# Gate logits and output projection with tokens as rows: 512 columns a product, bias folded in by split products

## The reference, cut to what matters

```
proj = rmsnorm(x, ln_mix_g) @ w_in            # q, k, v of two attentions, then ga, gb (1024 each)
o_a, o_b = attention a (512 wide), attention b (256 wide)
mix = sigmoid(ga + b_gate_a) * (o_a @ w_o_a) + sigmoid(gb + b_gate_b) * (o_b @ w_o_b)
x   = x + mix @ w_out
x   = x + moe_ffn(rmsnorm(x, ln_ffn_g))       # router, top 4 of 32 experts, gate/up/down products
return rmsnorm(x, ln_final_g)
```

## Time and profile before

| what | value |
| --- | --- |
| median of 3 executions | 1134.42 us (1134.16 to 1135.12) |
| the profiled execution | 1132.39 us, span of its instructions 1130.4 us |
| mean granted PE clock | 0.998 |
| busy | PE 97%, PE weight load 44%, DVE 28%, ACT 18%, POOL 2% |
| HBM read | 437.69 MB, 388 GB/s over the span |

### The profile page before, as it was taken

How to read it: one execution, slowest core, us unless ns; L and a number is a source line. 1 busy time by engine, 2 the same in 40 slices (tenths; PEclk the granted TensorE clock), 3 DMA queues, 4 the chain that set the end, 5 groups by cost and what they waited for, 6 DMA issues and landing times.

```text
span 1130.4 us, 12440 instructions
## 1 busy us (share of the span) xinstructions
PE 1094.6 (97%) x5385; PEld 496.0 (44%) x5385; DVE 315.7 (28%) x684; ACT 205.4 (18%) x367; POOL 19.6 (2%) x27
## 2 busy tenths in 40 slices
PE   8999999999999999999999999999999999999997
PEld 6888888733333333333333333333333333333332
DVE  7566778421111111111121111111111111111121
ACT  6445547210000000000110000000000000000011
POOL 1000110000000000000000000000000000000000
PEclk9999999999999999999999999999999999999999
DMA  9854229999999999999999999999999999999997
GB/s 360 264 181 156 110 78 407 408 403 429 427 435 419 430 428 427 432 428 431 430 429 431 429 432 427 431 431 430 432 430 433 428 432 430 434 431 430 426 427 286
DMA packets 38727, 439.23 MB, mean 389 GB/s; under 512 B 3050, under 2 KB 4482, under 8 KB 19748
## 3 DMA queue, kind: packets, MB, share of 16 engines
q1 hardware_dynamic: 38388, 438.41, 92.4%
q10 hardware_dynamic: 304, 0.33, 0.1%
HBM read 437.69 MB, written 1.05 MB: 388 GB/s over the span
## 4 chain that ended last, share of the span: by engine, by line
PE 72%; DMA 25%; DVE 1%; issue 1%; ACT 0%; SPq 0%; DVEq 0%; POOLq 0%; POOL 0%; ACTq 0%
PE ps L1150 42%; DMA pair<-in_w_up_dram 21%; PE ps L776 5%; PE ps L1174 5%; DMA pair<-in_w_down_dram 4%; PE ps L1080 3%; PE ps L878 2%; PE ps L806 2%; PE ps L814 2%; PE ps L931 1%; PE ps L1127 1%; PE ps L933 1%; PE ps L932 1%; PE ps L1019 1%; PE ps L1021 1%; PE ps L1020 1%
## 5 line engine op out<-in xcount | busy, mean ns | idle before, releaser
L1150 PE MATMUL ps<-pair,o_t 128*64 128x512 f32 x3072 | 681.0, 595 | 20.6 <-DMA pair<-in_w_gate_dram 16.8
L1150 PEld LDWEIGHTS ps<-pair,o_t 128*64 128x64 f32 x3072 | 215.9, 137 | 441.2 <-issue 408.0
L1624 DVE TENSOR_SCALAR work<-ps 128x512 f32<-128x512 f32 x32 | 22.1, 691 | 492.2 <-PE ps L1150 492.2
L710 ACT ACTIVATE o_t<-ps 128x512 f32<-128x512 f32 x32 | 19.1, 597 | 297.9 <-PE ps L776 297.9
L1174 PE MATMUL ps<-attn,o_t 64*128 64x512 f32 x256 | 71.5, 639 | 0.0
L697 ACT ACTIVATE attn<-work 128x512 f32<-128x512 f32 x32 | 20.1, 629 | 258.4 <-DVE work L1624 258.4
L1080 PE MATMUL ps<-xs,work 128*64 128x512 f32 x256 | 60.9, 593 | 0.0
L716 ACT ACTIVATE attn<-ps 128x512 f32<-128x512 f32 x31 | 18.5, 597 | 228.0 <-PE ps L1150 228.0
L776 PEld LDWEIGHTS ps<-cst,work 128*128 128x128 f32 (+1 forms) x294 | 35.8, 170 | 54.8 <-issue 52.1
L776 PE MATMUL ps<-cst,work 128*128 128x128 f32 (+1 forms) x294 | 53.0, 296 | 1.0 <-DVE work L1441 0.6
L1630 DVE TENSOR_SCALAR a_rows<-ps 128x512 f32<-128x512 f32 x32 | 22.1, 691 | 103.1 <-PE ps L1150 103.1
(11 more groups left out here) (184 smaller groups left out, 841.7 us busy)
## 6 DMA issues: line engine op xcount, KB each, us to landing
pair<-in_w_gate_dram SPq DMA_DIRECT2D x25, 4096.0 KB, 35.3
pair<-in_w_up_dram SPq DMA_DIRECT2D x25, 4096.0 KB, 34.5
pair<-in_w_down_dram SPq DMA_DIRECT2D x25, 4096.0 KB, 36.9
pair<-in_w_gate_dram SPq DMA_DIRECT2D x12, 2048.0 KB, 13.5
pair<-in_w_up_dram SPq DMA_DIRECT2D x12, 2048.0 KB, 15.3
pair<-in_w_down_dram SPq DMA_DIRECT2D x9, 2048.0 KB, 13.3
wd<-in_w_in_dram SPq DMA_DIRECT2D x5, 2048.0 KB, 9.1
wu<-in_w_in_dram SPq DMA_DIRECT2D x4, 2048.0 KB, 11.1
```

Of the source, the lines that this page charges most:

```text
L1150: mm = pe.matmul(ps[SLOTS * h:SLOTS * h + SLOTS, bank, :], lhs[:, k, :], ring[(at + j) % RING][:, r, 512 * h:512 * h + 512], start=(k == 0 ...
```

## The change

Gates: 8 outputs of 128 tokens by 512 gate columns in place of 16 of 128 columns by 256 tokens. Each is filled in two parts (`gate_part(u)`, 4 k steps each), so the place in the weave stays. ACT's emptying of PSUM applies 1/std of the token as its scale, in 8 instructions of 512 columns, after odd u only, and POOL's 16 multiplications go. Since the bias now varies along the columns, it goes in as a first product over 3 rows: std of the token (split hi, hi, lo) by bias (hi, lo, hi), which the later 1/std cancels. For that there are four new DMAs (broadcast to 32 rows each), one ACT copy after chunk 5, four DVE instructions ahead of the first gate, and the first gate waits for them.

Mixer: 4 outputs n of 128 tokens by 512 columns, in an order written out by hand; sigmoids are 4 instructions of 1024 elements. The mix must then be transposed, 4 PE transposes for each n (`turn_mixed`); ACT and DVE split it out of PSUM. Splits of the rows of `w_out` stand at other places of ACT's and DVE's order. The experts' biases are split at u = 2, not 8.

```diff
-            def evac_gate(t):
-                act.wait_ge(gate_done, t + 1)
-                act.activation(gates[:, t // KT, t % KT, :], ps[:, t % 2, 0:SEQ], ACT.Copy).then_inc(gate_read, 1)
+            def evac_gate(i):
+                c, b = i // NB, i % NB
+                act.wait_ge(gate_done, i + 1)
+                if i == 3:
+                    act.wait_ge(bias_lo_ready, 1)
+                act.activation(gates[:, 2 * (c % 2) + b, c // 2, :], ps[:, i % 2, :], ACT.Copy, scale=stat[:, 12 + b:13 + b])\
+                   .then_inc(gate_read, 1)
...
-                evac_gate(u)
+                if u % 2:
+                    evac_gate(u // 2)
...
-                if u == 8:
+                if u == 2:
                     split_biases()
...
-            act.wait_ge(gates_scaled, 16)
...
+            act.wait_ge(gate_read, 8)
             sigmoids(0)
             sigmoids(1)
             act.wait_ge(p_turned, N_UNITS)
             act.wait_ge(ld_wout[0], 16)
             split_row(0)
+            split_row(1)
             sigmoids(2)
...
+            mixed_hi(0)
+            mixed_hi(1)
+            sigmoids(3)
             act.wait_ge(ld_wout[1], 16)
+            act.wait_ge(mix_ready, 2)
             split_row(4)
...
+            def gate_part(u, ks):
+                i, c = u // 2, GATE_CHUNK0 + u // 4
+                b, bank = i % NB, i % 2
+                if ks[0] == 0:
+                    if i >= 2:
+                        pe.wait_ge(gate_read, i - 1)
+                    elif i == 0:
                         pe.wait_ge(proj_read, NB * 7)
+                        pe.wait_ge(gbias_ready, 4)
+                    at = 32 * (c - GATE_CHUNK0)
+                    pe.matmul(ps[:, bank, :], std_tab[at:at + 3, P * b:P * b + P], gbias_tab[at:at + 3, :], start=True, stop=False)
                 for k in ks:
+                    if k % 2 == 0 and b == 0:
+                        pe.wait_ge(hi_ready, PARTS * c + k // 2 + 1)
+                        pe.wait_ge(lo_ready, PARTS * c + k // 2 + 1)
+                    pe.matmul(ps[:, bank, :], h_hi[:, b, k, :], w_hi[:, c % 2, k, :], start=False, stop=False)
+                    pe.matmul(ps[:, bank, :], h_lo[:, b, k, :], w_hi[:, c % 2, k, :], start=False, stop=False)
+                    mm = pe.matmul(ps[:, bank, :], h_hi[:, b, k, :], w_lo[:, c % 4, k, :], start=False, stop=(k == KT - 1))
...
+                gate_part(2 * q, range(0, 4))
...
                 if q + 1 in LATE:
-                    gate_tile(2 * q + 1, range(0, 3))
+                    gate_part(2 * q + 1, range(4, 6))
                     scores(q + 1)
-                    gate_tile(2 * q + 1, range(3, KT))
+                    gate_part(2 * q + 1, range(6, KT))
...
+            def turn_mixed(n):
+                pe.wait_ge(mix_ready, n + 1)
+                for j in range(4):
+                    mm = turn(ps[:, TURNED[n], P * j:P * j + P], mix_rows[n][:, P * j:P * j + P])
+                mm.then_inc(mix_turned, 1)
...
             mixer_a(0)
+            mixer_a(1)
+            mixer_b(0)
+            mixer_b(1)
+            mixer_a(2)
+            turn_mixed(0)
+            turn_mixed(1)
+            mixer_b(2)
+            mixer_a(3)
+            turn_mixed(2)
+            mixer_b(3)
...
+                if k == 0:
+                    turn_mixed(3)
...
+                    dve.wait_ge(spread_ready, 1)
+                    dve.tensor_scalar(std_all, std_hi[:], cst[:, C_SGN + 2:C_SGN + 3], None, ALU.mult).then_inc(gbias_ready, 1)
+                    dve.wait_ge(spread_ready, 2)
+                    dve.tensor_scalar(gbias_s, gbias_hi[:], cst[:, C_SGN + 3:C_SGN + 4], None, ALU.mult).then_inc(gbias_ready, 1)
+                    dve.wait_ge(gbias_ready, 2)
+                    dve.scalar_tensor_tensor(std_tab[:], ps[:, 6, 0:SEQ], cst[:, C_SGN:C_SGN + 1], std_all, ALU.mult, ALU.add)\
+                       .then_inc(gbias_ready, 1)
+                    dve.scalar_tensor_tensor(gbias_tab[:], gbias_raw, cst[:, C_SGN + 1:C_SGN + 2], gbias_s, ALU.mult, ALU.add)\
+                       .then_inc(gbias_ready, 1)
...
-                if u == 8:
+                if u == 2:
                     dve.wait_ge(bias_hi_ready, 1)
...
+            mixed_a(0)
+            split_row(0)
+            mixed_a(1)
+            mixed(0)
+            mixed(1)
+            split_row(1)
+            mixed_a(2)
+            mixed_lo(0)
+            mixed_lo(1)
+            mixed(2)
+            split_row(4)
+            mixed_a(3)
+            mixed(3)
+            mixed_lo(2)
+            split_row(5)
+            split_row(2)
+            mixed_lo(3)
```

More of the change, by code:

```diff
@@ L408, in _ @@
             sp.dma_start(msk, masks).then_inc(ld_msk, 16)
+            for c in range(4):
+                of = (b_gate_a, b_gate_b)[c // 2][0:1, CHUNK * (c % 2):CHUNK * (c % 2) + CHUNK]
+                sp.dma_start(gbias_raw[32 * c:32 * c + 32, :], of.broadcast_to([32, CHUNK])).then_inc(ld_rows, 16)
             for part in range(2):
@@ L633, in _, with sigmoids, mixed_hi @@
             split_hi(N_CHUNKS + 1, 1)
-            act.wait_ge(gates_scaled, 16)
             evac_o(5)
             split_o(5, 6)
[L638 to L641, removed]
+            def sigmoids(n):
+                act.activation(gates[:, n, :, :], gates[:, n, :, :], ACT.Sigmoid).then_inc(gates_ready, 1)
             def split_row(k):
                 act.activation(wx_hi[k], wx_raw[:, k, :], ACT.Copy).then_inc(wx_hi_ready, 1)
+            def mixed_hi(n):
+                act.wait_ge(mix_turned, n + 1)
+                for to, at in turned_parts(n, mix_ha, mix_hb):
+                    act.activation(to, at, ACT.Copy).then_inc(mix_hi_ready, 1)
+            act.wait_ge(gate_read, 8)
             sigmoids(0)
@@ L982, in mixer_product @@
                 for k in tiles:
-                    pe.matmul(ps[:, MIX[m % 4], columns], wo_hi[:, k, P * m:P * m + P], o_hi[:, k, :],
-                              start=(k == tiles[0]), stop=False)
-                    pe.matmul(ps[:, MIX[m % 4], columns], wo_hi[:, k, P * m:P * m + P], o_lo[:, k, :], start=False, stop=False)
-                    mm = pe.matmul(ps[:, MIX[m % 4], columns], wo_lo[:, k, P * m:P * m + P], o_hi[:, k, :],
-                                   start=False, stop=(k == tiles[-1]))
@@ L988, in mixer_product @@
-                return mm
-            def mixer_a(m):
-                if m < 2:
-                    pe.wait_ge(gate_read, 15 + m)
-                elif m >= 4:
-                    pe.wait_ge(mix_ready, m - 3)
-                mm = mixer_product(m, range(0, 4), slice(0, SEQ))
-                if m == KT - 1:
-                    mm.then_inc(oproj_a_done, 1)
+                    pe.matmul(ps[:, bank, :], o_hi[:, k, cut], wo_hi[:, k, half], start=(k == tiles[0]), stop=False)
+                    pe.matmul(ps[:, bank, :], o_lo[:, k, cut], wo_hi[:, k, half], start=False, stop=False)
@@ new lines, in mixer_product, with mixer_a, mixer_b @@
+                    mm = pe.matmul(ps[:, bank, :], o_hi[:, k, cut], wo_lo[:, k, half], start=False, stop=(k == tiles[-1]))
+                return mm
+            def mixer_a(n):
+                if n == 0:
+                    pe.wait_ge(gate_read, 7)
+                elif n >= 2:
+                    pe.wait_ge(mix_a_used, n - 1)
+                mixer_product(n, range(0, 4), MIX[n % 2][0]).then_inc(oproj_a_done, 1)
+            def mixer_b(n):
+                if n == 0:
+                    pe.wait_ge(gate_read, 8)
+                    pe.wait_ge(lo_ready, PARTS * (N_CHUNKS + 1) + 2)
+                    pe.wait_ge(o_lo_ready, 2)
+                elif n == 1:
+                    pe.wait_ge(o_ready, 6)
+                else:
+                    pe.wait_ge(mix_ready, n - 1)
+                mixer_product(n, range(4, 6), MIX[n % 2][1]).then_inc(oproj_done, 1)
```

166 lines of the change are left out of this document (76 added, 90 removed).

## The result

The changed kernel takes 1141.16 us (median of 4, 1140.21 to 1141.90) where the kernel before takes 1134.29 in the same comparison: a ratio of 1.0062 (95% interval 1.0049 to 1.0074), 6.9 us slower. I had forecast 1135.8 and a range up to 1138.8. The profiled execution took 1140.99 us.

A forecast was written before the change was run, and what follows sets the result against it. The DMA weight stream sets the end, which follows the first expert product. Terms 0.3 (last gate) + 0.2 + 0.4 (mixer) + 0.5 (output product) = +1.4 us on 1134.42 gave 1135.8, range 1132.8 to 1138.8.

The forecast's parts named there:

- the DMA hides it: Rival: DMA backlog carries the PE's delay and only the last gate's +0.3 us counts, 1134.7; chance 0.1.
- the price of the bias product's neighbourhood: Gate tiles: weight change between the 3-row bias product and its neighbours, bounds 0 and 0.10 us, taken as 0.05.
- The wide product saves the cover of one load a tile: Gate tiles: a wide first product may cover the weight load, saving 0 to 0.1 us a tile, taken as 0.06.
- First gate +0.1: Four added DVE instructions, about 1.9 us together, make the first gate wait 0.1 us (0 to 0.6).
- Bias split +1.15: Units 2 and 3: DVE's bias split ahead of unit 3's division makes the scores of pair 3 1.15 us late.
- POOL's relief -0.53, up to -1.08 over two stretches: Scores 5 to 6: without POOL's work a slow DVE lo split gives back 0.53 us; possibly again after scores 7.
- Gate stage: First gate to last transposes: shifts from wide products, bias split and POOL's relief, +0.3 us at the last gate.
- my sum at scores 5: Cumulative shift of the PE at the scores of pair 5, first-gate wait included: +1.55 us.
- Mixer and output product +1.1 with the start: Last gate to first expert product: +0.2 emptying the gate, +0.4 mixer, +0.47 fourth transposes; no waits charged.
- a wait inside the mixer: Rival: late hand-overs between ACT and DVE in mixer or output product add 1.5 to 3 us, 1138; chance 0.22.
- The softmax chain runs ahead: Rival, gate stage: fewer ACT waits for gate tiles remove PE waits and hide the bias split, -2.6, 1131.9; chance 0.12.
- the bias products are dear: Rival: breaks around each of 8 bias products add at most 2.0 us, 1.3 with hidden ones off, 1137.1; chance 0.08.

The follow-up runs named there:

- fillers: Kernel before plus 12 more 512-column filler products just ahead of the first expert product: 1139.29 us.
- 128 rows: Changed kernel with its 8 bias products over all 128 table rows instead of 3 (wrong bias multiples): 1137.01 us, one run.
- before spread: Kernel before with the eight down-bias products in two groups of four, one expert apart: 1134.02 us.
- fillers spread: Kernel before with 12 more filler products ahead of the first expert product and the down-bias products in two groups of four: 1136.52 us.
- after spread: Changed kernel with the eight down-bias products in two groups of four: 1140.67 us.
- no POOL: Kernel before without POOL's 16 multiplications by 1/std, gates left unscaled: 1133.55 us, one run.
- zero-filled (3): Changed kernel, DVE split behind unit 3, 128-row bias products with zero-padded std tables: 1135.65 us; product last: 1135.58; also down biases in two groups: 1134.86.
- split at u = 3: Changed kernel with DVE's split of the experts' biases behind unit 3 instead of unit 2: 1139.20 us.
- no bias: Changed kernel without the 8 three-row bias products, gate biases missing from the result: 1137.64 us.
- bias last: Changed kernel with DVE's bias split behind unit 3 and the 3-row bias product last in each gate output: 1137.33 us.

## Why the prediction was wrong

**The frame held.** The DMA sets the end, and the end moves one to one with the first expert product: fillers +2.54 and +2.50. The rival "the DMA hides it" falls.

**The step that failed** is the price of the bias product's neighbourhood: "Against it stands a change of weights between the 3-row bias product and its neighbours, which no row shows; the bounds are 0 and that 0.10, I take 0.05." Measured, it is some 0.4 beside the product's own 0.24. And the sentence is wrong in itself: the trace of before does show products of few rows. In its chain, and in its weight loads (PEld), stand the down biases:

```profile
332.56 3.63 PE ps L1096 x8
336.19 0.42 PE ps L1127
```

```profile
333.46 0.18 PEld L1096 LDWEIGHTS ps<-attn,work 32*128 32x128 f32 x1 [0.24 <-issue]
333.89 0.18 PEld L1096 LDWEIGHTS ps<-attn,work 32*128 32x128 f32 x1 [0.24 <-issue]
...
336.12 0.19 PEld L1127 LDWEIGHTS ps<-bias_tab,pick_bias 128*128 128x128 f32 x1 [0.76 <-issue]
336.54 0.20 PEld L1150 LDWEIGHTS ps<-pair,o_t 128*64 128x64 f32 x4 [0.24 <-issue]
```

These products of 32 rows and 512 columns start 0.43 us apart, not 0.227: a load of 0.18, then 0.24 without a load, in turns. (They are two records for each product of float32 operands; the expert products are that too, with 128 rows, and start 0.22 apart, so it is not the type.) If a product of few rows between two of 128 rows has two such breaks of 0.2 us, that is 0.4 for each, or 0.35 more than I charged, some seven times: +2.4 us, from rows that were there. Measured from the kernel after to the one with 128 rows it is 2.72. Full rows alone do not cover a load: the 0.42 of the product at 336.19 comes from the load behind it, of 128 rows but 64 columns in place of 128 (336.54). That load is bare too, and so are the same loads at 501.95 and 511.29. A change of columns can therefore cost such a break as well. Whether the load behind a 3-row product is bare because of the few rows or because of the change of form, no run separates. I looked for the nearest row among the gate products, by place, instead of among products of few rows, by form.

The Trainium skill, "TensorE: Matmul & The Clock Gate", section "LDWEIGHTS (loading the stationary operand)", says that a load takes as long for 32 rows as for 128, and this trace agrees (means of 181 ns for 3 rows, 184 for 32 and 187 for 128). Its section "Why this matters for your kernels" gives a single product over 32 rows the time of one over 128; the records agree (587 ns for 32 rows, 592 for the expert products of 128). In a row of loads and products the trace does not bear this out, 0.43 against 0.227: the load is as long, but it is no longer covered.

**The other terms.**
- *The wide product saves the cover of one load a tile (0.06)*: it does not. The first wide product behind the transposes is followed 0.31 to 0.34 us later, some 0.10 over its pitch, with the bias product or without. With the term above, that makes +0.06 + 0.06 + 0.35 = +0.47 for an even part; measured +0.54 (transposes to scores 3.35 before, 106.78 to 110.67 = 3.89 after).
- *First gate +0.1*: about 0.2. The four added DVE instructions took 0.34, 0.48, 0.48 and 0.74, near the 0.35 to 0.65 assumed.
- *Bias split +1.15*: right in place and kind, measured 1.34.
- *POOL's relief -0.53, up to -1.08 over two stretches*: measured -0.68 alone. POOL's work was what slowed the two splits, as the rule on the shared interfaces had it (no run shows the interfaces themselves), but only the first lay on the path: between scores 7 and the last values nothing moved.
- *Gate stage*: 98.94 to 177.19 is 78.25, before 98.20 to 172.23 is 74.03. +4.2 where I had some +0.4. So the miss up to the first expert product lies here: my sum at scores 5 was +1.55, and with the start taken off it was 142.60 - 137.97 - 0.52 = +4.11. From there to the mixer I had -1.05 and it was +0.33; of that 1.38 the form with 3 rows takes 0.20 + 0.39 + 0.43 = 1.02 (last three rows of the table).
- *Mixer and output product +1.1 with the start*: from 36.52 to 37.32 us, +0.8, and last values to first mixer product 1.57 to 1.87, +0.3, with 0.34 idle. Right. The only wait of the PE between 177 and 214 us is that one, so the rival of a wait inside the mixer falls.

```profile
177.19 0.47 PE L1014 MATMUL ps<-w_hi,h_hi 128*128 128x512 f32 x1 [0.34 <-issue]
...
194.97 0.39 PE L1064 MATMUL ps<-wx_two,mix_ha 128*128 128x512 f32 x1
...
214.51 0.63 PE L804 MATMUL ps<-cst,xs 128*128 128x128 f32 x4
```

- *The softmax chain runs ahead*: it does not; the waits for `work` before transposes grew to 2.7 us and those before values stayed at 1.1.
- *The rival "the bias products are dear"* was the right one in kind. I gave it 0.08, and its "at most" of 0.25 each was below what the form costs. So the case was there and its price and chance were too small.

**The last 1.6 us** were in no step: the dips of the clock. Time of the profiled execution less the start of its first expert product separates the kernels:

| dip at 335 to 350 us | kernels | end less first expert product, us |
| --- | --- | --- |
| no | before, before spread, fillers spread, after spread, no POOL, zero-filled (3), 128 rows | 908.2 to 909.9, middle 909.3 |
| yes | after, split at u = 3, no bias, bias last, fillers | 910.2 to 911.8, middle 910.9 |

So the stretch's 5.24 and a dip's 1.6 make 6.8, and the medians differ by 6.87. This adds up roughly: the two profiled executions differ by 8.6, of which 0.5 is the start, 5.24 the stretch and 2.84 what lies behind it, since before's is the shortest of the nine. The kernel with fillers shows the price directly: spreading the eight products, and nothing else, took it from 1139.29 to 1136.52. Why the changed kernel has it so often stays open. Its four runs lie at mean clocks of 0.995 to 0.998; of the 57 runs of the kernel before for which the experiments list a clock, 13 were at 0.997 or less, and none of the 32 of the other kernels with the eight products spread, and the no-bias kernel, with a stretch of only +0.9, had the dip in its profile. So it is not the lateness by itself. The dips were seen behind products of 32 rows and behind a wait of the PE.

## What to carry to other kernels

Price an operation by the row that has its form, even if it stands 200 us away in another stage; a matmul over few rows between products of 128 rows cost two bare weight loads here (some 0.4 us beside 0.24 for 3 rows), and filling its rows with zeros took them away. Moving an engine's small job costs its full length if the engine's next result is what the PE waits for. Where a single run's end has to be compared, take it apart at the point where the bound changes, and look at the clock in small windows: a mean of 0.996 hid a loss of 1.6 us.

## What the hardware showed that I had not expected

- The weight load of a 3-row or 32-row product was not covered (PEld idle 0.17 to 0.24 us ahead of it), nor was the 128-row load behind a 3-row one, nor a load of 64 columns behind a product with 128; between products of 128 rows and 128 columns loads of 0.19 us were. Pitch 0.43 against 0.227 us.
- On this one core the granted clock falls for single stretches of a few microseconds in the middle of dense work, to 0.50 to 0.79 in the lowest 5 us window of each of five profiles, right behind eight products of 32 rows; here the kernel after:

```profile
338.26 3.69 PE L1143 MATMUL ps<-attn,work 32*128 32x512 f32 x8
341.88 0.51 PE L1174 MATMUL ps<-bias_tab,pick_bias 128*128 128x512 f32 x1
342.33 3.99 PE L1197 MATMUL ps<-pair,o_t 128*64 128x512 f32 x10
```

  There ten expert products take 3.99 us, 0.4 each, where they otherwise start 0.22 apart (7.02 us for 32). With the eight products issued four and four, the mean clock was 0.998 or more in all 32 runs of the three kernels other than the changed one.
